# Order and hold of the first loads of a two-block transformer kernel, and a shorter warm-up

## The reference, cut to what matters

```python
def first_block(x, p, g_mix, w_in, b_gate, ...):
    h = rmsnorm(x, g_mix[i])                       # x * rsqrt(mean(x*x) + EPS) * g
    z = jnp.einsum("bsd,dn->bsn", h, w_in[i])      # 1024 x 4608, in 36 units of 128 columns
    a_val, a_gt = z[..., :o1], z[..., o1:o2]
    ...                                            # convolutions, gates, w_a_out, w_b_out, w_o
    x = x + jnp.einsum("bsf,fd->bsd", f, w_down[i])
    x = x + pg * jnp.einsum("bsk,kd->bsd", p[i], w_ple[i])
    return rmsnorm(x, g_final)

def second_block(x, attn_pre_g, w_in, ...):        # attention, then a feed-forward with convolution
    ...
    return x + rms_norm(f, ffn_post_g[layer])
```

## Time and profile before

| | us |
|---|---|
| median of 3 runs | 752.59 (752.15 to 752.77) |
| the profiled execution's own time | 752.84 |
| its span, first to last instruction | 750.8 |
| PE busy | 743.0 (99% of the span) |
| DVE, ACT, POOL busy | 578.7, 452.0, 210.6 |
| granted TensorE clock, mean | 1.00 |

### The profile page before, as it was taken

How to read it: one execution, slowest core, us unless ns; L and a number is a source line. 1 busy time by engine, 2 the same in 40 slices (tenths; PEclk the granted TensorE clock), 3 DMA queues, 4 the chain that set the end, 5 groups by cost and what they waited for, 6 DMA issues and landing times.

```text
span 750.8 us, 16764 instructions
## 1 busy us (share of the span) xinstructions
PE 743.0 (99%) x5950; PEld 722.7 (96%) x5950; DVE 578.7 (77%) x1049; ACT 452.0 (60%) x765; POOL 210.6 (28%) x136
## 2 busy tenths in 40 slices
PE   9999999999999999999999999999999999999997
PEld 9999999999999999999999999999999999988885
DVE  6899986877887887434987794799999999973333
ACT  7645456556665665445765798876766666643431
POOL 0477642460000000343464003322112212212220
PEclk9999999999999999999999999999999999999999
DMA  8566553565555567544444344365555555666551
GB/s 307 182 217 205 184 166 127 197 201 195 194 180 189 190 204 250 198 162 152 159 161 139 115 134 125 111 199 200 192 190 195 180 184 196 210 212 193 186 179 56
DMA packets 37917, 135.48 MB, mean 180 GB/s; under 512 B 4464, under 2 KB 4720, under 8 KB 37872
## 3 DMA queue, kind: packets, MB, share of 16 engines
q1 hardware_dynamic: 37728, 134.86, 54.4%
q10 hardware_dynamic: 144, 0.00, 0.0%
HBM read 133.80 MB, written 1.05 MB: 180 GB/s over the span
## 4 chain that ended last, share of the span: by engine, by line
PE 89%; DVE 3%; ACT 3%; issue 2%; POOL 1%; DMA 1%; SPq 0%; DVEq 0%; POOLq 0%; ACTq 0%
PE bank L1901 25%; PE bank L1902 25%; PE bank L1903 25%; PE bank L2349 4%; PE bank L2348 4%; PE bank L2347 4%; DVE w_lo L1223 1%; ACT w_hi L787 1%; DMA raw<-in_w_in 1%; POOL X L755 1%; PE bank L2176 1%; ACT score L1079 0%; PE bank L2200 0%; PE bank L1959 0%; DVE sumsq L1813 0%
## 5 line engine op out<-in xcount | busy, mean ns | idle before, releaser
L1901 PE MATMUL bank<-h_hi,w_hi 128*128 128x256 f32 x1372 | 385.9, 281 | 0.3 <-DVE w_lo L1223 0.2
L1902 PE MATMUL bank<-h_lo,w_hi 128*128 128x256 f32 x1372 | 382.9, 279 | 0.0
L1903 PE MATMUL bank<-h_hi,w_lo 128*128 128x256 f32 x1372 | 382.8, 279 | 0.0
L787 ACT ACTIVATE w_hi<-raw 128x1024 fp32r<-128x1024 f32 (+2 forms) x243 | 258.9, 1068 | 93.2 <-PE bank L1903 41.3
L1223 DVE TENSOR_TENSOR w_lo<-raw,w_hi 128x1024 fp32r<-128x1024 f32 (+2 forms) x187 | 236.6, 1268 | 85.9 <-ACT w_hi L787 84.0
L1901 PEld LDWEIGHTS bank<-h_hi,w_hi 128*128 128x128 f32 x1372 | 257.9, 188 | 1.8 <-DVE w_lo L1223 0.7
L1902 PEld LDWEIGHTS bank<-h_lo,w_hi 128*128 128x128 f32 x1372 | 258.0, 188 | 0.0
L1903 PEld LDWEIGHTS bank<-h_hi,w_lo 128*128 128x128 f32 x1372 | 257.9, 188 | 0.0
L636 POOL TENSOR_TENSOR w_lo<-raw,w_hi 128x1024 fp32r<-128x1024 f32 (+1 forms) x56 | 139.0, 2485 | 382.9 <-ACT w_hi L787 374.7
L1281 DVE TENSOR_TENSOR bank<-bank,scales 128x256 f32<-128x256 f32 x116 | 49.5, 430 | 26.3 <-PE bank L1903 17.6
L1572 DVE SCALAR_TENSOR_TENSOR cg<-bank,vec,cg 128x255 f32<-128x255 f32 x108 | 51.5, 476 | 0.7 <-ACT cg L1019 0.6
(11 more groups left out here) (235 smaller groups left out, 963.2 us busy)
## 6 DMA issues: line engine op xcount, KB each, us to landing
raw<-in_w_up SPq DMA_DIRECT2D x108, 512.0 KB, 3.3
raw<-in_w_in SPq DMA_DIRECT2D x53, 512.0 KB, 3.4
raw<-in_w_down SPq DMA_DIRECT2D x32, 512.0 KB, 4.2
raw<-in_w_down SPq DMA_DIRECT2D x16, 704.0 KB, 4.2
raw<-in_w_o SPq DMA_DIRECT2D x8, 512.0 KB, 4.3
raw<-in_w_gate SPq DMA_DIRECT2D x8, 512.0 KB, 3.4
raw<-in_w_out SPq DMA_DIRECT2D x8, 512.0 KB, 3.3
raw<-in_w_b_out SPq DMA_DIRECT2D x4, 512.0 KB, 3.6
```

The lines of the kernel that those rows point to most:

```text
L787: nc.scalar.activation(hi_of(u)[:, cols], raw[s][:, cols], ACT.Copy).then_inc(hi_ready, 1)
L1901: nc.tensor.matmul(ps, wh, hi[:, k, :], start=start and n == 0, stop=False)
L1902: nc.tensor.matmul(ps, wh, lo[:, k, :], start=False, stop=False)
L1903: last = nc.tensor.matmul(ps, wl, hi[:, k, :], start=False, stop=stop and n == len(ks) - 1)
```

## The change

It reorders and holds loads at the start of the program on SP, moves one rounding and one remainder behind the next chunk pair on ACT and DVE, and drops three of sixteen warm-up products on PE.

```diff
-WARM_UP = 16
+WARM_UP = 13
...
             load_x(0)
             load_first(0, first_in)
             load_x(1)
+            load_x(2)
             load_first(1, raw_in[0])
-            load_x(2)
             load_x(3)
             load("in", 1, (1, None))
+            sp.wait_ge(raw_in[0], 16)
             load("in", 2, (2, None))
             sp.dma_start(ident[:], d["ident"]).then_inc(ident_in, 16)
             load("in", 3, (3, None))
...
-                if c == 3:
+                if c == 5:
                     act.wait_ge(raw_in[0], 16)
                     nc.scalar.activation(w_hi[0][:, first_half(1)], raw[0][:, first_half(1)], ACT.Copy
                                          ).then_inc(hi_ready, 1)
...
-                if c == 3:
+                if c == 5:
                     rest_of_first(1, (hi_ready, 1), lo_ready[0])
```

## The result

The changed kernel takes 754.02 us (median of 22 runs, 752.64 to 755.72), the kernel before takes 752.69 us in runs beside it (median of 22, 751.59 to 754.44). The ratio is 1.0018, with a 95% interval of 1.0011 to 1.0026: **slower by 1.3 us**, clear of no change, just inside the 0.2% that the prediction called the same. The forecast was 752.6 with a range of 751.8 to 753.2; the measured time lies outside it, 0.8 us past its upper end.

What follows compares the result with a forecast made beforehand. The prediction took unit 1's load, which sets when PE begins unit 1, as the bound, with units 2 and 3 following without a gap. Its terms, 0 + 0 + 0 + 0.05 us on 752.59, gave about 752.6, range 751.8 to 753.2.

Steps and rivals of the forecast that it cites:

- What bounds the kernel: Start of the program: unit 1's load, landing at 9.46 us, sets PE's start of unit 1 at 10.59; no pause follows.
- The two nearly due dates: DVE's remainder of unit 2 and last add of squares: 0.3 and 0.1 us of room before PE wants them.
- Three warm-up products less: PE's start: six fast passes go, first product moves from 7.21 to 6.54 us, but unit 1 waits for its load: worth 0.
- Swap and moved rounding: Unit 0's second half in fifth place: PE stands still from 7.95 to 9.1 us, ends unit 0 at 10.5, costs nothing.
- The hold speeds up nothing ahead of it: Load queue on SP: it serves in order, unit 2 was never ahead of unit 1, so no gain is taken.
- The rival of the freed queue: Queue from 4.5 to 7.5 us: holding later loads lands unit 1 near 8.75, PE starts it 0.45 us sooner, 752.15; chance 0.33.
- When unit 2 lands: Held load of unit 2: issued at 7.5, landing taken as 10.9 us against about 10.78 before; cost taken as 0.05 us.
- The bound from unit 1's landing: Unit 2's earliest landing: unit 1's 9.46 plus 524 KB at 395 GB/s, 1.33 us, gives 10.8.
- Unit 2 comes late: Rival: unit 2 lands at 11.8, PE waits at unit 2 and the squares, 1.0 us in all, 753.6; chance 0.12.
- Behind unit 2: Later loads: unit 4 comes 0.2 us later, covered by 0.8 us since its remainder waits for POOL's root.
- The fallen clock: Rival: PE's 1.15 us standstill from 7.95 us drops it to 1.2 GHz for 5.3 us, giving 755.1; chance 0.03.

## Why the prediction was wrong, point by point

*What bounds the kernel*: right. Unit 1's load sets when it begins, and behind it PE carries what is late to the end. The two nearly due dates were the ones that mattered: unit 2's remainder and the sum of squares. Both waits are in the profile after, 1.93 and 0.2 us.

*Three warm-up products less*: worth 0, right, as far as the ratio of 1.0002 without the hold can tell. When PE's level rises differs by execution: near 5.0 us in the profile after, so that the first product came at 5.96 and not at 6.54, and so late in the second execution of the change that all but the last of the 26 passes were slow.

*Swap and moved rounding*: right. PE stood still before unit 0's second half (1.19 us from start to start, 1.07 more than a product; forecast 1.15) and still ended unit 0 before unit 1 could begin.

*The hold speeds up nothing ahead of it*: right on the whole. Unit 1 was rounded at 9.3, 9.6, 8.9 and 9.2 in the change, at 9.5, 9.7 and 9.1 before: 0.2 us on average, and 9.2 and 8.8 in the two kernels that swap and hold nothing beyond 4.5 us. The rival of the freed queue had 0.33, too much. From 4.5 to 7.5 us the queue moved 343 to 365 GB/s in the four executions of the change, 300, 306 and 369 in the three of before, and 324 without the hold. The dip of the first trace is thus mostly one of that execution; what is left on average, 30 GB/s over 3 us, is 90 KB or 0.2 us, the size of what unit 1 gained. The Trainium skill's rule on HBM latency under load (DMA: Bandwidth & Descriptors, "Latency and other measured facts") was the rival's support; here a held and lighter queue landed unit 1 sooner by no more than those 0.2 us.

*When unit 2 lands*: **this is the step that failed**. I put 7.5 plus 3.1 to 3.5, "since nothing else is on the way by then", and took 10.9. The issue was right (7.0 to 7.7), the duration was not: 4.8 us on average over the four executions of the change, from 4.3 to 5.7. The premise "since nothing else is on the way by then" contradicts my own sum, which lands unit 1 at 9.46, two microseconds after the issue. And the row I took the median of, 3.5, mixes states of the queue. Its 17 loads, sorted by how long the load before had still to go at the issue (from the trace before, issue and landing of each):

| the load before has still to land for, us | time to landing, us |
|---|---|
| nothing | 3.1 |
| 0.1 to 0.9 | 3.1, 3.1, 3.2, 3.2, 3.2, 3.3, 3.5; one took 6.2 |
| 1.4 to 2.5 | 3.3, 3.9, 4.0, 4.3, 4.4 |
| 3.0 to 4.0 | 4.3, 5.1, 5.3 |

The held load is one of the third line (unit 1 had 1.9 to 2.2 us to go): 3.3 to 4.4 us, median 4.0, would have put the landing at 11.5 and the cost at 0.6 us. Two of the four executions took that line's 4.3; the other two, 4.9 and 5.7, took more than any of it, for which no run shows the cause. The bound from unit 1's landing, 10.8, treated its tail as a queue at full rate. The Trainium skill's fit of 2.0 us plus bytes at 436 GB/s (DMA: Bandwidth & Descriptors, "Anatomy of one DMA"), which that section gives for loads issued by GpSimd and not by SP, made it 3.2 us and was short by 1.6 us on average. The row's other end, 6.2, stood in the text, and 13.7 with it, but the price of the step was taken from its middle alone.

*Unit 2 comes late*, the rival with 0.12, is what happened: its mechanism, its place (PE paused at 13.4), the second wait at the squares, and roughly its rule, one for one from a landing of 10.9 (landings 1.9, 1.7, 0.4 and 0.6 us past it, unit 2 late by 1.9, 1.2, 0.7 and 0.7 us behind unit 1). It forecast 753.6; measured 754.0. Its chance was too small because I gave one value to a term whose row spread from 3.1 to 6.2 while the room was 0.1 us.

*Behind unit 2*: unit 4 came not 0.2 but 2.9 us later (18.52 for 15.59), from a queue at 262 to 284 GB/s. The cover of 0.8 us held only because the root, which it waits for, had moved with unit 2; where the hold was longer the cover broke and PE paused there as well.

*The fallen clock*, at 0.03, did not come in the change, but see below.

## What to carry to other kernels

In this kernel a wait on the issuing queue did not delay a load by the wait alone: it took away its place in a full queue, and the load then paid its whole latency, here 4.3 to 5.7 us, where in the kernel before it landed 1.3 us behind its forerunner. A load's time to landing must be taken from rows in the same state of the queue, and where the spread of those rows is larger than the room at the place where it is due, the spread is the forecast. Here the loads landed in the order of issue, and holding the later ones gained those ahead 0.2 us at most; what is due soon belongs into the queue early.

## What the runs showed of the hardware that was not expected

**A slower pace of TensorE at full clock.** In one of the executions of the kernel before, the products of the first feed-forward stage start 117.8 ns apart for 170 us on end, 116.7 in the two others, with a granted clock of 1.00 in all three. The stretches of the two (us, busy of PE with its count, PEld, DVE, ACT, POOL, clock, DMA share, GB/s), the slower one first:

```profile
180.00:240.00 60.00, 60.00 (x512) 60.00 (x511) 48.41 (x85) 35.77 (x54) 0.00 (x0) 1.00 0.57 191
...
500.00:560.00 60.00, 60.00 (x517) 60.00 (x516) 59.37 (x106) 41.26 (x67) 14.46 (x6) 1.00 0.59 196
```

```profile
180.00:240.00 60.00, 60.00 (x516) 60.00 (x515) 49.01 (x86) 36.21 (x54) 0.00 (x0) 1.00 0.57 192
...
500.00:560.00 60.00, 60.00 (x517) 60.00 (x516) 59.27 (x105) 41.28 (x67) 14.30 (x6) 1.00 0.58 193
```

512 instead of 516 products in 60 us are 0.8%; from start to start it is 0.95%, or 1.6 us over the stage. In later stages the two executions run alike. The slow pace was seen in other stretches too (40 to 110 us in the kernel with the hold behind unit 2, and in the one that delays the small loads), in five of seventeen executions in all, and it is as large as the effect under study. It comes without the hold as well, and in none of the four executions of the change, so it is not its cost. Together with the spread near 137 us it explains a part of why single executions of one kernel differ by up to 3 us, and why a ratio needs many of them. What starts it is open.

**The clock fell after a pause of 2.9 us.** Where nothing was issued behind unit 2, PE paused before unit 4 and then ran at its 1.2 GHz level: its weight load came after

```profile
24.03 0.19 PEld L1903 LDWEIGHTS bank<-h_hi,w_hi 128*128 128x128 f32 x1 [2.90 <-DVE w_lo L1225]
```

and the stretches behind it, with the granted clock in the third column from the end, show products 0.21 us apart and then 0.12 us apart again (a count takes in what only reaches into the stretch):

```profile
24.00:27.40 3.40, 3.37 (x17) 3.37 (x18) 3.00 (x8) 3.33 (x7) 2.39 (x1) 0.56 0.54 174
28.00:30.00 2.00, 2.00 (x19) 2.00 (x18) 1.75 (x5) 1.25 (x3) 1.61 (x1) 1.00 0.78 254
```

The level was still the full one when PE went on at 24.03, fell 0.4 us later and was back at 27.8. That cost about 1.6 us beside the pause (16 products at 0.1 us more). The other execution of this kernel shows the same after 2.7 us, with the fall 0.8 us behind the restart and 3.4 us at the lower level. The pauses of up to 1.9 us in the change and with the longer hold left the clock at 1.00. The forecast's rival was right in kind, with too long a stay at the lower level (5.3 us for 3.4); the pause that it had in mind, 1.1 us in the change, did not bring the clock down.
